# Column sums of squares: sixteen accumulating matmuls or vector additions and one matmul, and the order of the first weight split

## The chip, the cores and the metric

The kernel runs on one core of a Trainium2 chip. The metric is the device time of one execution in microseconds (us), the median of repeated runs. Five engines run side by side, each through its own list of instructions: TensorE (PE) multiplies matrices into the accumulation banks (PSUM, eight banks), VectorE (DVE) and ScalarE (ACT) work element by element, GpSimd (POOL) too, and SyncE (SP) issues the transfers. They wait for each other by semaphores alone. The profile tells a matmul (PE) from the load of its stationary operand (PEld).

## The reference, cut to what matters

Two layers of a decoder trunk, for a prompt of 1024 tokens and 8 sample tokens, so 1032 token columns in all; model width 1024, hidden width 2816:

```
def rmsnorm(x, g):
    y = x * lax.rsqrt(jnp.mean(x * x, axis=-1, keepdims=True) + EPS)
    return y * g

for layer in range(2):
    h = rmsnorm(x, norm_mix_pre[layer])
    mix = mixer(h) @ w_out                       # layer 0: gMLP and DeltaNet, layer 1: differential attention
    x = x + rmsnorm(mix, norm_mix_post[layer])
    h = rmsnorm(x, norm_ffn_pre[layer])
    f = (gelu(conv(h @ w_gate) + b) * (h @ w_up)) @ w_down
    x = x + rmsnorm(f, norm_ffn_post[layer])
```

Activations are kept transposed, width on the 128 partitions (8 row blocks of 128) and tokens along the free dimension. So the mean over the width in `rmsnorm` is a sum over partitions: a matmul of the squares with a matrix of ones, here called a column sum. It leaves the sum in each of the 128 partitions.

## The kernel before

All of it is written engine by engine: the order of each engine's instructions is the order of the code, and no scheduler moves anything. The 1032 tokens are cut into three thirds of 344 columns (`CH`). Each product of 32-bit matrices is made of three matmuls, high half by high half, high by low and low by high; so each operand is split once into a rounded copy (`..._hi`, ScalarE) and the remainder (`..._lo`, VectorE).

The diff touches one function, `stage_out_ffn`, which runs once per layer. Its parts:

1. The output projection of the mixer. `out_unit(c, m)` makes one 128 x 344 unit (third c, row block m) from 24 matmuls. Before it the input and the weights are split: `input_hi` and `input_lo` take one block of one third, `weight_hi` and `weight_lo` one weight tile of 128 x 1024. The first unit waits for weight tile 0 and, block by block, for the input.
2. Both norms and the gate and up projections of the first group, then eleven groups of the hidden width in a loop.
3. The last group, by thirds. `end_unit(n)` makes unit n (n = 0 to 23, eight per third) of the down projection from 6 matmuls; `end_collect(n)` adds it on VectorE to the sum in `T.acc`; `end_square(n)` squares it on ScalarE; `end_sum(n)` is its column sum, three units later (`LAG`), accumulated over the eight blocks. `end_root(c)` makes the reciprocal root on ScalarE (a logarithm and an exponential, each with a load of its function table), and `end_renew(c, k)` on VectorE scales block k and adds the old x, two instructions.
4. In layer 0 alone (`queries is not None`): the next norm and the query projection of layer 1. `end_square_x` squares the new x, `end_sum_x` takes its column sums, `end_root2` the root; `end_input(c)` scales and splits a third (a scaling and a remainder per block on VectorE, the copy `end_hi` on ScalarE), and `query(q)` makes unit q of 24 from 24 matmuls. `move_query(q)` empties its bank. Queries 8 to 15 read the second third, 16 to 23 the last.
5. In layer 1 alone (`closing`): `turn_out` transposes the result on TensorE, ScalarE copies it out of PSUM and SyncE stores it. This is the end of the kernel.

A column sum of 344 columns stands in the program as one matmul of `T.con` (the ones) with a square; in the trace it has two rows of PE (L1222). Each of the 24 units of part 3 has such a sum, and each of the 24 blocks of part 4.

## Time and profile before

| | us |
|---|---|
| runs | 3087.94, 3082.85, 3080.01 |
| median | 3082.85 |
| the profiled execution | 3086.49 |
| its span, first to last instruction | 3084.7 |
| TensorE busy | 2900.4 |
| VectorE busy | 1522.8 |
| ScalarE busy | 1034.2 |

The page of the profile gives the busy time of each engine and, in 40 slices of about 77 us, where it is busy. TensorE is at 9 tenths or more in most slices, and its granted clock (a share of full speed, 2.4 GHz) has a mean of 0.97. The end of layer 0 (parts 3 and 4) lies from 1528 to 1678 us of the span, the end of layer 1 from 3023 us to the last instruction; the two output projections begin at 680 and 2175 us. In a timeline the first number is the start in us from the start of the span, the second the time in us, then engine, line and operation with its operands, and in square brackets the idle time before it and what ended that.

### The profile page before, as it was taken

The numbers are of one execution on the slowest core, as the hardware profiler recorded it, in microseconds if no ns is written. First come the engines' busy times: TensorE is split into PE (matmuls) and PEld (weight loads), VectorE is DVE, ScalarE is ACT, GpSimd is POOL, SyncE is SP. The second block draws the span as 40 slices with busy tenths as digits, with TensorE's granted clock in tenths as the row PEclk, the third lists the DMA queues.
The fourth block names the chain that finished last, engine by engine and source line by source line (L and its number), as shares of the span: only waits on it lengthen the run. The fifth ranks groups of instructions, "written<-read, shape, count | busy, mean of one in ns | idle before, by whom it ended". The sixth has DMA issues, their size and how long they took to land. (4 is left out here: it accounts for less than half of the span.)

```text
span 3084.7 us, 46174 instructions
## 1 busy us (share of the span) xinstructions
PE 2900.4 (94%) x18588; PEld 2775.9 (90%) x18588; DVE 1522.8 (49%) x2258; ACT 1034.2 (34%) x1747; POOL 586.7 (19%) x322
## 2 busy tenths in 40 slices
PE   6999989969999999999998999996899999999997
PEld 5999888849899999999978888885899999999996
DVE  3067333356744444444471576773566444444435
ACT  3326544335511111111261566663462111111114
POOL 1122135200222222222100121210003222222210
PEclk8999989969999999999999999997999999999999
DMA  4111100043311111111131222213431111111103
GB/s 151 47 43 30 38 1 0 1 112 107 108 55 41 41 41 41 54 54 48 37 110 37 62 84 76 69 55 125 130 109 42 56 52 54 41 41 41 41 14 112
DMA packets 183498, 185.02 MB, mean 60 GB/s; under 512 B 10469, under 2 KB 168549, under 8 KB 183296
## 3 DMA queue, kind: packets, MB, share of 16 engines
q1 hardware_dynamic: 183380, 183.45, 19.0%
q8 instruction: 74, 1.21, 0.2%
q14 instruction: 44, 0.36, 0.0%
HBM read 151.13 MB, written 32.57 MB: 60 GB/s over the span
## 5 line engine op out<-in xcount | busy, mean ns | idle before, releaser
L1530 DVE TENSOR_TENSOR acc<-acc,ps 128x1032 f32<-128x1032 f32 x144 | 177.0, 1229 | 231.9 <-PE ps L124 231.9
L1911 PE MATMUL ps<-mix_in0hi,in0wh 128*128 128x344 f32 x600 | 197.8, 330 | 14.9 <-POOL mix_in0lo L244 9.1
L124 PE MATMUL ps<-midlo,rest0wh 128*128 128x344 f32 x984 | 209.3, 321 | 0.0
L124 PE MATMUL ps<-mix_out1lo,rest1wh 128*128 128x344 f32 x984 | 209.2, 321 | 0.0
L124 PE MATMUL ps<-midhi,rest0wl 128*128 128x344 f32 x984 | 208.8, 321 | 0.0
L124 PE MATMUL ps<-mix_out1hi,rest1wh 128*128 128x344 f32 x984 | 208.7, 320 | 0.0
L124 PE MATMUL ps<-midhi,rest0wh 128*128 128x344 f32 x984 | 208.7, 320 | 0.0
L124 PE MATMUL ps<-mix_out1hi,rest1wl 128*128 128x344 f32 x984 | 208.6, 320 | 0.0
L1911 PE MATMUL ps<-mix_in0hi,in0wl 128*128 128x344 f32 x600 | 193.1, 322 | 0.0
L1911 PE MATMUL ps<-mix_in0lo,in0wh 128*128 128x344 f32 x600 | 193.1, 322 | 0.0
L124 PEld LDWEIGHTS ps<-midhi,rest0wl 128*128 128x128 f32 x984 | 165.7, 188 | 0.0
L124 PEld LDWEIGHTS ps<-mix_out1hi,rest1wl 128*128 128x128 f32 x984 | 165.6, 188 | 0.0
L124 PEld LDWEIGHTS ps<-mix_out1lo,rest1wh 128*128 128x128 f32 x984 | 165.5, 188 | 0.0
L124 PEld LDWEIGHTS ps<-midhi,rest0wh 128*128 128x128 f32 x984 | 165.5, 188 | 0.0
L124 PEld LDWEIGHTS ps<-midlo,rest0wh 128*128 128x128 f32 x984 | 165.4, 188 | 0.0
L124 PEld LDWEIGHTS ps<-mix_out1hi,rest1wh 128*128 128x128 f32 x984 | 165.4, 188 | 0.0
L2884 PE MATMUL ps<-midhi,at_wh 128*128 128x344 f32 x384 | 133.1, 347 | 20.0 <-POOL at_wl L3252 9.2
L1911 PEld LDWEIGHTS ps<-mix_in0hi,in0wh 128*128 128x128 f32 x600 | 114.0, 190 | 18.5 <-issue 9.0
L383 POOL TENSOR_TENSOR rest0wl<-wraw,rest0wh 128x1024 fp32r<-128x1024 f32 x40 | 96.4, 2410 | 165.7 <-ACT rest0wh L379 165.5
L383 POOL TENSOR_TENSOR rest1wl<-wraw,rest1wh 128x1024 fp32r<-128x1024 f32 x40 | 96.1, 2404 | 166.4 <-ACT rest1wh L379 166.1
L2884 PE MATMUL ps<-midlo,at_wh 128*128 128x344 f32 x384 | 124.5, 324 | 0.0
L2884 PE MATMUL ps<-midhi,at_wl 128*128 128x344 f32 x384 | 124.5, 324 | 0.0
(496 smaller groups left out, 7060.7 us busy)
## 6 DMA issues: line engine op xcount, KB each, us to landing
wraw<-in_w_ffn_gate SPq DMA_DIRECT2D x22, 1024.0 KB, 5.1
wraw<-in_w_ffn_up SPq DMA_DIRECT2D x22, 1024.0 KB, 5.1
wraw<-in_w_ffn_down SPq DMA_DIRECT2D x22, 1024.0 KB, 4.8
wraw<-x_scratch SPq DMA_DIRECT2D x96, 172.0 KB, 3.1
x_scratch<-acc SPq DMA_DIRECT2D x72, 172.0 KB, 3.1
wraw<-in_w_in_even SPq DMA_DIRECT2D x24, 512.0 KB, 3.8
wraw<-in_w_in_odd SPq DMA_DIRECT2D x24, 512.0 KB, 4.8
sr_page<-in_cache_k SPq DMA_DIRECT2D x16, 512.0 KB, 4.0
```

The lines of the kernel that those rows point to most:

```text
L124: ins = pe.matmul(ps[:, 3 * r + c, 0:CH], w, h[:, c * CH:(c + 1) * CH], start=first and n == 0, stop=last and n == 2)
L383: pool.tensor_tensor(self.slot_l[j], self.source(j), self.slot_h[j], ALU.subtract).then_inc(self.lo[j], 1)
L1530: dve.tensor_tensor(a, a, region(T.ps, m % 2), ALU.add).then_inc(collected, 1)
L1911: ins = pe.matmul(bank(n, c), w[n % 2][:, k, :], cut(h[:, k, :], c), start=first and m == 0, stop=final and m == 2)
L2884: ins = pe.matmul(unit_bank, x[b][:, k, :], y[:, k, c * CH:(c + 1) * CH], start=k == 0 and m == 0, stop=k == KD - 1 and m == 2)
```

## The change

Three things are changed.

First, the squares of the first two thirds of the down projection (parts 3, both layers) are no longer summed by eight accumulating matmuls each. ScalarE writes the square of block 0 into a buffer `sum1[c]`, VectorE adds the squares of blocks 1 to 7 to it (`end_add`), and TensorE makes one column sum, `end_sum(0)` after unit 10 and `end_sum(1)` after unit 19. The last third keeps its eight sums, now called `end_last`.

Second, the same for the second and third third of the next norm in layer 0 (`end_add_x`, then `end_sum_x(1)` after query 4 and `end_sum_x(2)` after query 10; before they stood, eight each, after queries 3 and 6). The first third keeps its eight sums (`end_first_x`); its last one now stands ahead of the last three of `end_last`. On ScalarE and VectorE the squares, the weight splits and the moves around them are put in another order.

Third, in the output projection of both layers the first weight tile is split ahead of the input, and the second after input block 3.

A branch that no call takes (`not by_thirds`) is removed with its helper objects.

```diff
-            x_sq = [sum1[0], sum1[1]] + end_sq
+            x_sum, x_sq = [None, end_sq[0], end_sq[1]], [end_sq[2], end_sq[3], sum1[0], sum1[1]]
+            x_first = scaled
...
             @block.scalar
                 def end_square(n):
                     c, m = divmod(n, KD)
                     act.wait_ge(moved, NX + n + 1)
-                    if n >= 4:
-                        act.wait_ge(post_made, 3 + n - 3)
-                    act.activation(end_sq[n % 4], cut(T.acc, m, c), ACT.Square).then_inc(squared, 1)
+                    if c < 2 and m == 0:
+                        dst = sum1[c]
+                    else:
+                        dst = end_sq[n % 4]
...
+                        elif n >= 4:
+                            act.wait_ge(added, 21 + adds_until(n - 4))
+                    act.activation(dst, cut(T.acc, m, c), ACT.Square).then_inc(squared, 1)
...
+                weight_hi(0)
                 for k in range(KD):
                     input_hi(k, 0)
-                weight_hi(0)
-                weight_hi(1)
+                    if k == 3:
+                        weight_hi(1)
...
                     for k in range(KD):
                         end_hi(0, k)
+                    for k in range(4):
+                        end_square_x(1, k)
                     for m in range(4, KD):
                         query_hi(m)
+                    for k in range(4, KD):
+                        end_square_x(1, k)
                     end_root(2)
-                    for k in range(KD):
-                        end_square_x(1, k)
-                    for q in range(3):
+                    for q in range(2):
                         move_query(q)
                     end_root2(1)
...
             @block.tensor
+                def end_sum(c):
+                    if c == 0:
                         pe.wait_ge(keep_moved, 6)
+                    pe.wait_ge(added, 21 + 7 * c + 7)
+                    ones(end_post[c], sum1[c]).then_inc(post_made, 1)
...
+                def end_sum_x(c):
+                    pe.wait_ge(rooted2, 3 + c)
+                    pe.wait_ge(x_added, X_ADDS + 7 * c)
+                    ones(second, x_sum[c]).then_inc(second_made, 1)
...
+                for n in range(NX):
+                    end_unit(n)
+                    if n == 10:
+                        end_sum(0)
+                    if n == 19:
+                        end_sum(1)
+                    if n >= 2 * KD + LAG:
+                        end_last(n - 2 * KD - LAG)
+                    if queries is not None and n > 2 * KD:
+                        end_first_x(n - 2 * KD - 1)
                 if queries is not None:
-                    end_sum_x(0, KD - 1)
+                    end_first_x(KD - 1)
+                for m in range(KD - LAG, KD):
+                    end_last(m)
+                if queries is not None:
                     for q in range(NX):
                         query(q)
-                        if q in (3, 6):
-                            for k in range(KD):
-                                end_sum_x(q // 3, k)
+                        if q == 4:
+                            end_sum_x(1)
+                        if q == 10:
+                            end_sum_x(2)
...
             @block.vector
+                def end_add(n):
+                    c, m = divmod(n, KD)
+                    if m == 0:
+                        return
+                    dve.wait_ge(squared, NX + n + 1)
+                    if m > 1:
+                        dve.wait_ge(added, 21 + 7 * c + m - 1)
+                    dve.tensor_tensor(sum1[c], sum1[c], end_sq[n % 4], ALU.add).then_inc(added, 1)
...
+                weight_lo(0)
                 for k in range(KD):
                     input_lo(k, 0)
-                weight_lo(0)
-                weight_lo(1)
+                    if k == 3:
+                        weight_lo(1)
...
+                for n in range(2 * KD):
+                    end_collect(n)
+                    if n >= LAG:
+                        end_add(n - LAG)
+                for k in range(KD):
+                    end_renew(0, k)
+                    end_collect(2 * KD + k)
+                    if k < LAG:
+                        end_add(2 * KD - LAG + k)
...
+                    for k in range(1, 4):
+                        end_add_x(1, k)
                     for m in range(4, KD):
                         query_lo(m)
-                    for k in range(KD):
+                    for k in range(4, KD):
+                        end_add_x(1, k)
+                    for k in range(5):
                         end_renew(2, k)
                     end_input(1)
+                    for k in range(5, KD):
+                        end_renew(2, k)
+                    for k in range(1, KD):
+                        end_add_x(2, k)
                     end_input(2)
```

How the rows move, at three places. TensorE in layer 0, last group, before: a column sum (L1222; the squares lie in `ffn0gate`) after each unit of six matmuls (L1305, the last of one unit and all of the next are shown).

```order
L1305 MATMUL ps<-rest0wh,rest0wl 128x344
L1222 MATMUL ps<-ffn0gate,con_sb 128x344 [waits ev_cv_moved]
L1305 MATMUL ps<-rest0wh 128x344 [waits ev_cv_turned]
L1305 MATMUL ps<-rest0wl,rest0wh 128x344
L1305 MATMUL ps<-rest0wh,rest0wl 128x344
L1305 MATMUL ps<-rest0wh 128x344
L1305 MATMUL ps<-rest0wl,rest0wh 128x344
L1305 MATMUL ps<-rest0wh,rest0wl 128x344
L1222 MATMUL ps<-ffn0conv,con_sb 128x344 [waits ev_cv_moved]
```

The same place now, around unit 10: the end of unit 10, the one sum of the first third (L1224, of `sqsum`, where `sum1` lies), unit 11 (L1307) and the start of unit 12.

```order
L1307 MATMUL ps<-rest0wh,rest0wl 128x344
L1224 MATMUL ps<-sqsum,con_sb 128x344 [waits ev_mixed_made,ev_w_masked]
L1307 MATMUL ps<-rest0wh 128x344 [waits ev_turned]
L1307 MATMUL ps<-rest0wl,rest0wh 128x344
L1307 MATMUL ps<-rest0wh,rest0wl 128x344
L1307 MATMUL ps<-rest0wh 128x344
L1307 MATMUL ps<-rest0wl,rest0wh 128x344
L1307 MATMUL ps<-rest0wh,rest0wl 128x344
L1307 MATMUL ps<-rest0wh 128x344 [waits ev_turned]
```

No sum stands between units 11 and 12 now; the one that is left waits for VectorE's additions, where each of before waited for ScalarE's square.

VectorE at the same stage, before: `end_collect` (L1553), then the renewals (L1560, L1563).

```order
L1590 TENSOR_TENSOR rest0wl<-wraw,rest0wh 128x1024 [waits gd_s_updated1] x2
L1553 TENSOR_TENSOR acc<-acc,ps 128x344 [waits ev_mix_own] x16
L1560 TENSOR_TENSOR acc<-acc,ffn0conv 128x344 [waits ev_n_summed]
L1563 SCALAR_TENSOR_TENSOR acc<-acc,gain,wraw 128x344 [waits ev_n_logged,ev_col_in]
L1553 TENSOR_TENSOR acc<-acc,ps 128x344 [waits ev_mix_own]
L1560 TENSOR_TENSOR acc<-acc,ffn0conv 128x344
```

And now, from the last collections of the second third on (L1564 collects, L1573 adds a square, L1586 and L1589 renew).

```order
L1564 TENSOR_TENSOR acc<-acc,ps 128x344 [waits ev_v_normed]
L1573 TENSOR_TENSOR sqsum<-sqsum,ffn0gate 128x344 [waits ev_mixed_made,ev_vt_moved]
L1586 TENSOR_TENSOR acc<-acc,ffn0conv 128x344 [waits ev_mix_own]
L1589 SCALAR_TENSOR_TENSOR acc<-acc,gain,wraw 128x344 [waits ev_cv_turned,ev_n_summed]
L1564 TENSOR_TENSOR acc<-acc,ps 128x344 [waits ev_v_normed]
L1573 TENSOR_TENSOR sqsum<-sqsum,ffn0gate 128x344 [waits ev_mixed_made,ev_vt_moved]
L1586 TENSOR_TENSOR acc<-acc,ffn0conv 128x344
```

After each collection there is now an addition, also between the first three renewals and the next collection.

VectorE at the start of the output projection of layer 0, before: eight input remainders of the first third (L1444), then three weight remainders (L1547).

```order
L1440 UNCONDITIONAL_BRANCH [waits barrier_Pool_Activation_PE_DVE_SP_release]
L1444 TENSOR_TENSOR midlo<-acc,midhi 128x344 [waits ev_mixed_made] x8
L1547 TENSOR_TENSOR rest0wl<-wraw,rest0wh 128x1024 [waits ev_turned] x3
L1444 TENSOR_TENSOR midlo<-acc,midhi 128x344 [waits ev_mixed_made] x2
L1451 COPY acc<-ps 128x344 [waits ev_mix_moved,ev_mix_own]
```

And now (L1558 is the weight remainder, L1455 that of the input).

```order
L1451 UNCONDITIONAL_BRANCH [waits barrier_Pool_Activation_PE_DVE_SP_release]
L1558 TENSOR_TENSOR rest0wl<-wraw,rest0wh 128x1024 [waits ev_v_squared]
L1455 TENSOR_TENSOR midlo<-acc,midhi 128x344 [waits ev_v_logged] x4
L1558 TENSOR_TENSOR rest0wl<-wraw,rest0wh 128x1024 [waits ev_v_squared]
L1455 TENSOR_TENSOR midlo<-acc,midhi 128x344 [waits ev_v_logged] x4
L1558 TENSOR_TENSOR rest0wl<-wraw,rest0wh 128x1024 [waits ev_v_squared]
```

The same three weight remainders and eight input remainders stand there, with one weight remainder ahead of the first input block; ScalarE's copies are ordered alike.

## Rows read from the trace of the kernel before

**Rows 1.** the page, part 1: busy time of each engine
```profile
PE 2900.4 (94%) x18588; PEld 2775.9 (90%) x18588; DVE 1522.8 (49%) x2258; ACT 1034.2 (34%) x1747; POOL 586.7 (19%) x322
```

**Rows 2.** timeline of TensorE, queries of layer 0; start us, busy us, what
```profile
1593.04 1.32 PE L1222 MATMUL ps<-sqsum,con_sb 128*128 128x344 f32 x4
1594.19 1.90 PE L1222 MATMUL ps<-ffn0gate,con_sb 128*128 128x344 f32 x6
```

**Rows 3.** timeline of VectorE, last group of layer 0
```profile
1529.23 0.51 DVE L1553 TENSOR_TENSOR acc<-acc,ps 128x344 f32<-128x344 f32 x1
1530.17 0.51 DVE L1553 TENSOR_TENSOR acc<-acc,ps 128x344 f32<-128x344 f32 x1 [0.43 <-PE ps L1305]
...
1533.59 0.52 DVE L1553 TENSOR_TENSOR acc<-acc,ps 128x344 f32<-128x344 f32 x1 [1.01 <-PE ps L1305]
1535.12 0.51 DVE L1553 TENSOR_TENSOR acc<-acc,ps 128x344 f32<-128x344 f32 x1 [1.01 <-PE ps L1305]
...
1550.77 0.51 DVE L1560 TENSOR_TENSOR acc<-acc,ffn0conv 128x344 f32<-128x344 f32 x1
...
1551.86 0.51 DVE L1553 TENSOR_TENSOR acc<-acc,ps 128x344 f32<-128x344 f32 x1
1552.29 0.51 DVE L1560 TENSOR_TENSOR acc<-acc,ffn0conv 128x344 f32<-128x344 f32 x1
...
1566.70 0.51 DVE L1553 TENSOR_TENSOR acc<-acc,ps 128x344 f32<-128x344 f32 x1 [1.17 <-PE ps L1305]
...
1572.55 0.58 DVE L1573 SCALAR_TENSOR_TENSOR ffn0spare<-acc,gain,sqsum 128x344 f32<-128x344 f32 x1 [1.19 <-ACT sqsum L141]
```

**Rows 4.** timeline of ScalarE, last group of layer 0
```profile
1567.24 0.49 ACT L1025 ACTIVATE ffn0conv<-acc 128x344 f32<-128x344 f32 x1 [0.91 <-DVE acc L1553]
1567.75 1.28 ACT L140 ACT_TABLE_LOAD   x1
1570.17 0.55 ACT L140 ACTIVATE sqsum<-ps,eps 128x344 f32<-128x344 f32 x1 [1.13 <-PE ps L1222]
...
1572.03 0.49 ACT L141 ACTIVATE sqsum<-sqsum 128x344 f32<-128x344 f32 x1
```

**Rows 5.** timeline of TensorE, first query of layer 0
```profile
1574.35 0.48 PE L1338 MATMUL ps<-midhi,rest0wh 128*128 128x344 f32 x1 [4.22 <-DVE midlo L1578]
```

**Rows 6.** timeline of ScalarE, later queries of layer 0
```profile
1632.67 0.46 ACT L1066 ACTIVATE acc<-ps 128x344 f32<-128x344 f32 x1 [3.31 <-PE ps L1338]
```

**Rows 7.** who waited for whom, 1527 to 1700 us: total, times, longest
```profile
DVE ffn0spare L1573 <- ACT sqsum L141: 10.3, 3, 7.4
```

**Rows 8.** timeline of VectorE, last group of layer 1
```profile
3024.05 0.51 DVE L1553 TENSOR_TENSOR acc<-acc,ps 128x344 f32<-128x344 f32 x1 [2.72 <-PE ps L1305]
...
3057.34 0.51 DVE L1553 TENSOR_TENSOR acc<-acc,ps 128x344 f32<-128x344 f32 x1
```

**Rows 9.** timeline of ScalarE, start of the output projection of layer 0
```profile
679.88 3.15 ACT L904 ACTIVATE midhi<-acc 128x344 fp32r<-128x344 f32 x8 [16.59 <-PEq L2682]
...
692.64 1.04 ACT L908 ACTIVATE rest0wh<-wraw 128x1024 fp32r<-128x1024 f32 x1
```

**Rows 10.** timeline of VectorE, the same stretch
```profile
684.01 3.50 DVE L1547 TENSOR_TENSOR rest0wl<-wraw,rest0wh 128x1024 fp32r<-128x1024 f32 x3
...
693.72 1.23 DVE L1547 TENSOR_TENSOR rest0wl<-wraw,rest0wh 128x1024 fp32r<-128x1024 f32 x1 [1.51 <-ACT rest0wh L908]
694.86 0.94 DVE L1444 TENSOR_TENSOR midlo<-acc,midhi 128x344 fp32r<-128x344 f32 x2
...
720.20 1.16 DVE L1457 TENSOR_TENSOR sqsum<-sqsum,ffn0gate 128x344 f32<-128x344 f32 x2
```

**Rows 11.** timeline of TensorE, the same stretch
```profile
685.29 0.66 PE L1237 MATMUL ps<-midhi,rest0wh 128*128 128x344 f32 x1 [14.26 <-DVE rest0wl L1547]
...
690.05 0.49 PE L1237 MATMUL ps<-midlo,rest0wh 128*128 128x344 f32 x1
690.33 0.38 PE L1237 MATMUL ps<-midhi,rest0wl 128*128 128x344 f32 x1
```

More of the change, by code:

```diff
@@ L758, in stage_out_ffn @@
         was_scaled, n_hi, n_lo, x_out, act_own = sem("was_scaled"), sem("n_hi"), sem("n_lo"), sem("x_out"), sem("act_own")
-        by_thirds = closing is not None or queries is not None
+        X_ADDS = 14
         BANKS, LAG = (6, 3) if queries is None else (5, 3)
@@ L764, in stage_out_ffn @@
         end_bank = lambda n: T.ps[:, bank_of(n), 0:CH]
+        adds_until = lambda n: 7 * (n // KD) + n % KD
         end_sq = [third(gate[:, 2:2 + TOK], n) for n in range(3)] + [third(conv, 0)]
@@ L851, in _ @@
                 sp.wait_ge(x_out, 16 * NX)
-                if not by_thirds:
-                    sp.wait_ge(keep_moved, 1)
-                    sp.dma_start(out_prompt[layer, 0], kept_rows[0:2, :]).then_inc(out_done, 16)
-                    sp.dma_start(out_sample[layer, :, 1, :], kept_rows[2:KEEP, :]).then_inc(out_done, 16)
-                    sp.wait_ge(out_done, 48)
-                else:
-                    if queries is not None:
-                        for j in range(feed.SLOTS):
-                            sp.wait_ge(lo[j], GROUPS)
-                        queries.first(sp)
-                    sp.wait_ge(keep_moved, 6)
-                    for cols, src in rows:
-                        sp.dma_start(out_prompt[layer, 0][:, cols], src[0:2, :]).then_inc(out_done, 16)
-                        sp.dma_start(out_sample[layer, :, 1, cols], src[2:KEEP, :]).then_inc(out_done, 16)
-                    sp.wait_ge(out_done, 80)
-                    for n in range(4):
-                        load_end_x(n)
+                if queries is not None:
+                    for j in range(feed.SLOTS):
+                        sp.wait_ge(lo[j], GROUPS)
+                    queries.first(sp)
+                sp.wait_ge(keep_moved, 6)
+                for cols, src in rows:
+                    sp.dma_start(out_prompt[layer, 0][:, cols], src[0:2, :]).then_inc(out_done, 16)
+                    sp.dma_start(out_sample[layer, :, 1, cols], src[2:KEEP, :]).then_inc(out_done, 16)
+                sp.wait_ge(out_done, 80)
+                for n in range(4):
+                    load_end_x(n)
                 if queries is not None:
@@ L1212, in _ @@
                 group(GROUPS - 1, False)
-                if not by_thirds:
-                    pool.memset(T.sqsum[:], 0.0).then_inc(sqsum_own, 1)
-                    for m in range(KD):
-                        squares.gpsimd(pool, m // 2, m % 2, lambda: pool.wait_ge(
-                            *((squares.summed[(m - 1) % 2], (m + 1) // 2) if m else (sqsum_own, 1))))
             @block.tensor
@@ L1403, in _ @@
                 pe.wait_ge(gate_in, 2 * GROUPS)
-                if by_thirds:
-                    pe.wait_ge(multiplied, 2 * GROUPS)
-                else:
-                    down(GROUPS - 1, 2 * GROUPS)
-                    pe.wait_ge(collected, KD * GROUPS)
+                pe.wait_ge(multiplied, 2 * GROUPS)
                 pe.wait_ge(kept, 2 * GROUPS)
@@ L1650, in _ @@
                     group(g, True)
-                if not by_thirds:
-                    collect(GROUPS - 1)
-                    dve.wait_ge(keep_turned, 1)
-                    dve.tensor_copy(kept_rows, flat[:, 0:FF]).then_inc(keep_moved, 1)
-                else:
-                    if queries is not None:
-                        query_lo(2)
-                        query_lo(3)
-                    for n in range(2 * KD):
-                        end_collect(n)
-                    for k in range(KD):
-                        end_renew(0, k)
-                        end_collect(2 * KD + k)
+                if queries is not None:
+                    query_lo(2)
+                    query_lo(3)
+                for n in range(2 * KD):
[7 more added lines that the diff above has]
+                        end_add(2 * KD - LAG + k)
                 if queries is not None:
```

107 lines of the change are left out of this document (52 added, 55 removed).

## The prediction

> **What bounds the kernel now.** I read the page first, then the timeline of each engine alone in the four stretches that the change touches, then the waits of the second half of layer 0. On the page TensorE is busy 94% of the span and VectorE 49% [rows 1]: time taken off TensorE counts wherever no other engine takes its place. What one column sum costs TensorE is to be read from starts, since recorded times overlap: four rows of L1222 take 1594.19 - 1593.04 = 1.15 us, so a row is 0.289 us and a sum of two rows 0.58 us [rows 2]. In the last group VectorE's collections follow TensorE's units: 1530.17 - 1529.23 = 0.94 us apart while no sum stands between, 1.52 us once one does, each with about 1 us of VectorE idle until TensorE is done [rows 3]. So there TensorE sets the pace and VectorE has room.
>
> **The first two thirds of the last group (both layers).** Removed: 16 sums, added 2, in each layer. Added on VectorE: 14 additions of 344 columns per layer. The trace has that operation beside a collection: from 1551.86 to 1552.29 the next instruction starts 0.43 us after a collection, while its recorded time is 0.51 us [rows 3]. I price collection plus addition at 2 x 0.43 = 0.86 us, under TensorE's 0.94. The bounds of one addition are 0.43 us and the 1.16 - 0.51 = 0.65 us by which the second of two dependent additions ends behind the first elsewhere; I take 0.43, since here a collection stands between two additions. The Trainium skill ("VectorE: DVE Perf Modes", Terms) says that a flush follows every VectorE operation and the next can't issue until the pipe is empty. By that rule a pair would cost 1.02 us and the units would be paced by VectorE; the rows' 0.43 us between starts says that most of the recorded tail is overlapped, and the measurement decides.
>
> Now the chain, counted from the start of the first collection. Before, the renewals begin at 1550.77 - 1529.23 = 21.5 us [rows 3]. After: 15 units of 0.945 are 14.2 us; the sum of the first third stands behind unit 10 and waits for the addition of block 7, which VectorE makes after collecting unit 10. TensorE stands there for one collection and one addition (0.43 + 0.51) and hand-overs of some 0.2 us (estimate), 1.2 us, and then needs 0.58. The last collection and addition take 0.86. Sum 16.8 us: 4.7 us earlier. Squares of units 11 to 15 wait behind ScalarE's root as before and are in time for their additions.
>
> **The last third, layer 0.** Before, from the first renewal to the last collection: 1566.70 - 1550.77 = 15.9 us [rows 3]. A renewal (two instructions) and a collection take VectorE 1552.29 - 1550.77 = 1.52 us. Now the first three steps hold an addition too, 1.95 us each, and the sum of the second third (behind unit 19) waits for the last of these, at 5.9 us. From there TensorE has three sums (1.7 us), three units with two sums each (0.94 + 1.16 = 2.1 us each, 6.3), the last unit (0.94), 0.6 us for the root of the second third that holds up ScalarE's squares, and 0.2 to the collection: 15.7 us. So only 0.2 us is gained: what the missing sums save, the wait for VectorE takes.
>
> Behind the last collection ScalarE squares, loads a table, takes the logarithm, loads, takes the exponential, and VectorE begins the next input 5.85 us after the collection. In it ScalarE waits 1.13 us for TensorE's last sum, since sums of the down projection stand ahead of it [rows 4]. Now that sum stands ahead of them and is made while the table is loaded; the chain is 0.54 + 0.49 + 1.28 + 0.56 + 1.30 + 0.52 = 4.7 us, 1.1 us less. The pause of TensorE ahead of the first query (4.22 us) [rows 5] shrinks a little and takes the three moved sums. Layer 0 reaches its queries 4.7 + 0.2 + 1.1 = 6.0 us earlier.
>
> **The queries of layer 0.** 24 units of 24 matmuls, 3.31 + 0.46 = 3.77 us each [rows 6], TensorE never waiting after the first one. Sixteen sums become two: 14 x 0.58 = 8.1 us, if the later thirds are in time. VectorE gets 14 more additions, back to back, at most 0.65 us each, 9.1 us. Against them stand 10.3 us in which it waited here for ScalarE's root, 7.4 at once ahead of the last third [rows 7]. Worked through: the second third's squares are summed some 4 us before query 4 ends; sum 0.6 and root 2.5 us later VectorE makes the second input, its first block 7 us before query 8 reads it and its last (8.5 us later) while query 8 runs, which needs that block only at its end. The last third has about 5 us to spare at query 10. I cost the reordering on ScalarE at nothing: its moves of queries stay within the five banks by one query or more at every place.
>
> **The last third, layer 1.** The last collection comes at 3057.34 - 3024.05 = 33.3 us, the next renewal 0.43 later, 33.7 [rows 8]. No sum of a next norm stands here, and VectorE is the pace of this third already (1.52 us per step, no idle time). After: 16.8 us as above, three steps of 1.95 and five of 1.52: 30.3 us. Gain 3.4 us, though TensorE is relieved of 8.1. ScalarE's last root, the copies out and the stores hang on the last collection and move with it.
>
> **The first weight tile (both layers).** ScalarE's first copy starts at 679.88; a weight copy takes 1.04 us and hands over 1.08 us after its start [rows 9]. VectorE makes three weight remainders at 684.01, behind eight input remainders; one weight remainder holds it for 694.86 - 693.72 = 1.14 us [rows 10]. TensorE starts at 685.29, 5.41 us after ScalarE [rows 11]. Now: 1.08 (weight copy), 1.14 (weight remainder), 0.52 (first input remainder), 0.05: 2.8 us, so 2.6 us earlier. Behind it: the second weight remainder comes after input block 3, so block 4 is ready 2.9 us after the first; TensorE, slow here, needs three matmuls of 690.33 - 690.05 = 0.28 us per block [rows 11], 3.4 us for four, and does not catch up. SyncE's transfer of weight tile 4, which waits for the first remainder, is issued about 3 us earlier, behind the six small loads that stand ahead of it. The total work of VectorE and ScalarE up to unit 1 is the same, and TensorE is the pace of the rest of this part, so the lead lasts. The bounds are 0 and 2.6 us; the value is the second, as every handed-over time has a row. Layer 1 begins alike: 2 x 2.6 = 5.2 us.
>
> TensorE's clock: the first matmuls here run at the lower level (1.2 GHz), until about 690.3, 5.0 us after the first, behind a pause of 14 us [rows 11]. If the rise stays at its old moment instead of moving with the first matmul, the 2.6 us that are won run at half speed and are worth 1.3. The Trainium skill ("TensorE: Matmul & The Clock Gate", Part 1) calls the half rate the default that activity releases: by that rule the rise moves along, and the sum stays.
>
> **Sum.** 6.0 + 8.1 + 3.4 + 5.2 = 22.7 us. The profiled execution took 3086.49 us with a span of 3084.7, so its like would be 3063.8 and 3062.0. It is 3.6 us above the median of the runs (3082.85); against the median the forecast is 3060.2 us, 0.7% faster.
>
> **The rivals.**
>
> A, VectorE becomes the pace of the first two thirds: an addition costs 0.65 us instead of 0.43. For: the two dependent additions at 720.20 [rows 10]. Against: they stand back to back. Price: pair 1.08 us against 0.945 on 13 units and 0.22 in three steps, 2.4 us per layer: gain 17.9, time 3065.
>
> B, the early first tile gives half or nothing (clock, or a wait behind it): 2.6 to 5.2 us less, 3062.8 to 3065.4.
>
> C, a later third is late at query 8 or 16, because VectorE or ScalarE is held up (a store or load of x, a table load): TensorE waits there. For: fourteen additions and a longer chain ahead of the input. Against: the slack above. Price up to the 8.1 us of that term: 3068.
>
> D, the other side: the new pauses of TensorE (1.2 us behind unit 10, 0.8 and 0.4 ahead of the first two sums of the next norm, 0.8 behind unit 19) let its clock fall at the end of layer 0 and it is not raised again before the queries are through. A query then takes 24 x 0.28 = 6.8 us instead of 3.8. It decides from 22.7 / 3.0 = 7.6 queries at the lower level; over all 24 it costs 72 us, time 3132. Against: behind the far longer pause of 14 us the lower level lasted 5.0 us [rows 11], and the pause ahead of the first query that is there already, 4.22 us [rows 5], is longer than any new one and no query behind the first is slow [rows 6].
>
> E, it doesn't do what it says: the sums' time was hidden somewhere I took for exposed, and half of the gain is missing or less: 3071 to 3083. Against: the 1.52 against 0.94 us of rows 3.
>
> **Chances.** The forecast (3057 to 3063) 0.66, A 0.10, B 0.08, C 0.06, D 0.03, E 0.04, more than forecast (all 42 removed sums count, 24.3 + 5.2 = 29.5 us, 3053) 0.03. The range is 3053 to 3069: from that bound up to C with the scatter of the runs. Less than 0.3% (9.2 us) can hardly be told from no change here; faster than that are all cases but D, E and a part of C: 0.92. Within it 0.05, slower 0.03.
>
> **What would show it.** The collections of units 1 to 10 start 0.95 us apart, with under 0.1 us of VectorE idle between; a single pause of TensorE of about 1.2 us ahead of the sum of the first third; the next input begins 4.7 us after the last collection; no idle time of TensorE from query 1 on, and its busy time about 24 us lower; the first matmul 2.8 us after ScalarE's first copy; from first to last collection in layer 1 29.9 us instead of 33.3. Wrong would be: collections 1.1 us apart (A), a pause ahead of query 8 or 16 (C), a granted clock under 0.9 in the queries (D).

## The result, and the profile after

The changed kernel takes 3059.34 us (median of 4 runs, 3056.90 to 3064.17), the kernel before 3082.56 us on the same chip (4 runs, 3080.01 to 3087.94). The ratio is 0.9925 (95% interval 0.9912 to 0.9937), 0.75% faster; the forecast was 3060.2 us. A second set of 5 runs gave 3058.11 us, ratio 0.9927 (0.9914 to 0.9941). The profiled execution has a span of 3062.3 us, against 3084.7 before.

The page's first part (engine, busy us, share of the span, instructions) answers to [rows 1]:

```profile
PE 2877.0 (94%) x18504; PEld 2759.3 (90%) x18504; DVE 1539.4 (50%) x2300; ACT 1033.4 (34%) x1747; POOL 586.7 (19%) x322
```

TensorE is busy 23.4 us less, VectorE 16.6 us more. The shares hardly move; where the time went is seen only in the stages.

The last group of layer 0, from VectorE's timeline (start, duration, engine, line, operation; in brackets the idle time before and what ended it). L1564 is a collection, L1573 an addition, L1586 the first half of a renewal, L1599 the scaling that begins the next input. It answers to [rows 3].

```profile
1527.67 0.51 DVE L1564 TENSOR_TENSOR acc<-acc,ps 128x344 f32<-128x344 f32 x1 [0.17 <-PE ps L1307]
...
1536.23 0.51 DVE L1564 TENSOR_TENSOR acc<-acc,ps 128x344 f32<-128x344 f32 x1
1536.66 0.51 DVE L1573 TENSOR_TENSOR sqsum<-sqsum,ffn0gate 128x344 f32<-128x344 f32 x1
1537.16 0.51 DVE L1564 TENSOR_TENSOR acc<-acc,ps 128x344 f32<-128x344 f32 x1
1537.59 0.51 DVE L1573 TENSOR_TENSOR sqsum<-sqsum,ffn0conv 128x344 f32<-128x344 f32 x1
1540.05 0.51 DVE L1564 TENSOR_TENSOR acc<-acc,ps 128x344 f32<-128x344 f32 x1 [1.95 <-PE ps L1307]
...
1544.67 0.51 DVE L1586 TENSOR_TENSOR acc<-acc,ffn0conv 128x344 f32<-128x344 f32 x1
...
1546.56 0.51 DVE L1586 TENSOR_TENSOR acc<-acc,ffn0conv 128x344 f32<-128x344 f32 x1
...
1560.42 0.51 DVE L1564 TENSOR_TENSOR acc<-acc,ps 128x344 f32<-128x344 f32 x1 [1.20 <-PE ps L1307]
...
1565.16 1.06 DVE L1599 SCALAR_TENSOR_TENSOR ffn0spare<-acc,gain,sqsum 128x344 f32<-128x344 f32 x2
```

From the fifth collection on there is one every 0.94 us with an addition between, and VectorE is not idle; the pace is still TensorE's (a collection starts within 0.05 us of the end of its unit's last matmul). Then comes one hole, in which TensorE waited for the addition of block 7 (1537.59) and made the sum and unit 11. TensorE's timeline has that pause, and the two that matter later:

```profile
1538.25 0.82 PE L1224 MATMUL ps<-sqsum,con_sb 128*128 128x344 f32 x2 [1.12 <-DVE sqsum L1573]
...
1566.95 0.39 PE L1348 MATMUL ps<-midhi,rest0wh 128*128 128x344 f32 x1 [3.09 <-DVE midlo L1604]
...
3028.16 0.84 PE L1224 MATMUL ps<-sqsum,con_sb 128*128 128x344 f32 x2 [2.92 <-DVE sqsum L1573]
```

ScalarE at the end of that group, and at the last query, answers to [rows 4] and [rows 6]. The root (L140) no longer waits for a sum: no bracket stands behind it.

```profile
1560.97 0.49 ACT L1026 ACTIVATE ffn0conv<-acc 128x344 f32<-128x344 f32 x1 [0.91 <-DVE acc L1564]
1561.48 1.28 ACT L140 ACT_TABLE_LOAD   x1
1562.77 0.55 ACT L140 ACTIVATE sqsum<-ps,eps 128x344 f32<-128x344 f32 x1
...
1613.40 0.55 ACT L140 ACTIVATE sqsum<-ps,eps 128x344 f32<-128x344 f32 x1 [4.98 <-PE ps L1224]
...
1662.43 0.46 ACT L1072 ACTIVATE acc<-ps 128x344 f32<-128x344 f32 x1 [3.31 <-PE ps L1348]
```

The output projection of layer 0: ScalarE's first copy, VectorE's first remainder, TensorE's first and first fast matmul, VectorE's first collection. It answers to [rows 9 to 11].

```profile
681.18 1.06 ACT L903 ACTIVATE rest0wh<-wraw 128x1024 fp32r<-128x1024 f32 x1 [16.58 <-PEq L2716]
682.27 1.22 DVE L1558 TENSOR_TENSOR rest0wl<-wraw,rest0wh 128x1024 fp32r<-128x1024 f32 x1 [5.75 <-ACT rest0wh L903]
684.07 0.63 PE L1239 MATMUL ps<-midhi,rest0wh 128*128 128x344 f32 x1 [11.73 <-DVE midlo L1455]
688.23 0.38 PE L1239 MATMUL ps<-midhi,rest0wl 128*128 128x344 f32 x1
690.05 0.52 DVE L1462 COPY acc<-ps 128x344 f32<-128x344 f32 x1
```

The last group of layer 1 on VectorE (first collection, first renewal, last collection), against [rows 8]:

```profile
3005.36 0.51 DVE L1564 TENSOR_TENSOR acc<-acc,ps 128x344 f32<-128x344 f32 x1 [2.73 <-PE ps L1307]
...
3022.36 0.51 DVE L1586 TENSOR_TENSOR acc<-acc,ffn1conv 128x344 f32<-128x344 f32 x1
...
3035.13 0.51 DVE L1564 TENSOR_TENSOR acc<-acc,ps 128x344 f32<-128x344 f32 x1
```

Stage by stage, in us, each from one mark to the next in the two traces:

| stage | before | after | gain | forecast |
|---|---|---|---|---|
| layer 0, ScalarE's first copy to first collection of the last group | 849.35 | 846.49 | 2.86 | 2.6 |
| layer 0, that collection to the next input | 43.32 | 37.49 | 5.83 | 6.0 |
| layer 0, next input to last query's move | 105.39 | 97.27 | 8.12 | 8.1 |
| layer 1, first copy to first collection of the last group | 849.21 | 846.27 | 2.94 | 2.6 |
| layer 1, first to last collection | 33.29 | 29.77 | 3.52 | 3.4 |

The five gains are 23.3 us (forecast 22.7). What isn't in the table was not changed: layer 0's projection begins 1.3 us later than before (681.18 against 679.88), attention is 0.24 us shorter, the end 0.14. 23.3 - 1.3 + 0.4 = 22.4 us, the difference of the spans.

### The profile page after: what moved, and what is told of

It reads as the page before. It is cut to its first block and busy times, and to the rows that moved or that the text cites. A ratio compares the mean times of both kernels' runs of the same rounds, so it can differ in the third digit from the quotient of the medians.

```text
span 3062.3 us, 46088 instructions
## 1 busy us (share of the span) xinstructions
PE 2877.0 (94%) x18504; PEld 2759.3 (90%) x18504; DVE 1539.4 (50%) x2300; ACT 1033.4 (34%) x1747; POOL 586.7 (19%) x322
## 5 line engine op out<-in xcount | busy, mean ns | idle before, releaser
L2918 PE MATMUL ps<-midhi,at_wh 128*128 128x344 f32 x384 | 132.7, 346 | 22.4 <-ACT at_vin L3044 11.3
```

Source lines behind the costliest of these rows:

```text
L2918: ins = pe.matmul(unit_bank, x[b][:, k, :], y[:, k, c * CH:(c + 1) * CH], start=k == 0 and m == 0, stop=k == KD - 1 and m == 2)
```

## The experiments

Every kernel below was timed in 5 rounds (the second addition in 3), and its ratio is to the kernel before on the same chip. The ratios carry an uncertainty of about 0.15%, 4 to 5 us. Differences smaller than that are read from marks in the traces, inside a stage, where the same stage of two profiled executions of the changed kernel agrees within 0.1 us. Across the untouched parts they don't: these two executions have spans of 3062.3 and 3054.1 us, and most of the 8 us lie between the last query of layer 0 and layer 1's projection (496.7 against 490.1 us).

**The first weight tile alone**, on the kernel before (ScalarE; VectorE's part is alike):

```diff
+                weight_hi(0)
                 for k in range(KD):
                     input_hi(k, 0)
-                weight_hi(0)
-                weight_hi(1)
+                    if k == 3:
+                        weight_hi(1)
```

> The kernel before with only the first weight tile split ahead of the input, on ScalarE and on VectorE, in both layers. My theory: TensorE's first matmul comes 2.6 to 2.9 us earlier behind ScalarE's first copy in each layer and the lead lasts, 5.2 to 5.9 us in all, so about 3077 us (ratio 0.998). Rival B (the early tile gives half or nothing, since the rise of TensorE's clock keeps its moment or a wait stands behind): 3080 to 3083, ratio 0.999 to 1.000.

Measured: 3077.18 us, ratio 0.9979 (0.9970 to 0.9988). From ScalarE's first copy to the first collection of the last group the trace has 846.61 us in layer 0 and 846.38 in layer 1, 2.74 and 2.83 less than before, 5.6 in all. The theory holds and rival B falls: the lead lasts over more than 800 us. What becomes of the clock's rise when the first matmul comes sooner is taken up again with the halves below.

**The changed kernel without it:** the same lines taken back.

> The changed kernel with the input split ahead of the first weight tile again, as before. My theory: it loses the 5.2 to 5.9 us of the early tile and nothing else, about 3065 us (ratio to the kernel before 0.9942), and the parts add up: its gain and that of the early tile alone sum to the whole gain of 23.2 us. Rival B: no slower than the changed kernel, 3059 to 3062. A rival for the sum: the parts overlap, and the two gains add up to clearly more or less than 23 us.

Measured: 3067.84 us, ratio 0.9952 (0.9939 to 0.9966). By the medians it loses 8.5 us, more than expected but within the uncertainty; by the trace 2.91 us in layer 0 (849.40 against 846.49 us). The gains of the two parts (6.3 and 15.6 us) sum to 21.9 us, against 23.2 us for the whole: within the uncertainty they add up.

**The query sums again:**

```diff
                         if q == 10:
                             end_sum_x(2)
+                        if q in (4, 10):
+                            for _ in range(7):
+                                ones(end_post[1], T.con[:, 0:CH])
```

> The changed kernel, with seven column sums more on TensorE behind each of queries 4 and 10 of layer 0 (of constants, into a bank that nobody reads): TensorE gets back the 14 sums that the change took from the queries, while VectorE keeps its additions. My theory: TensorE is the pace of the queries throughout, each sum is 0.58 us, so 8.1 us slower than the changed kernel, 3067.5. Rival C (VectorE's chain of additions, root and input is late somewhere, so that TensorE waited there anyway): less than 8.1 us is lost, about 3 to 6. Rival E (the sums had been hidden): 3059 to 3062.

Measured: 3071.79 us, ratio 0.9962 (0.9949 to 0.9976). The two marks in its trace, VectorE's next input and ScalarE's last move of a query:

```profile
1565.63 1.07 DVE L1602 SCALAR_TENSOR_TENSOR ffn0spare<-acc,gain,sqsum 128x344 f32<-128x344 f32 x2
...
1671.01 0.46 ACT L1072 ACTIVATE acc<-ps 128x344 f32<-128x344 f32 x1 [3.31 <-PE ps L1348]
```

105.38 us, where the changed kernel has 97.27 and the kernel before had 105.39. The 14 sums cost 8.11 us, 0.58 each, wholly exposed: rivals C and E fall. The median lost 12 us (11 by the two ratios); what goes beyond 8.1 lies in untouched parts (2.1 us of it in the profiled execution, between the queries and layer 1) or in the scatter.

**One more addition on VectorE**, eleven times in each layer:

```diff
+                    if n <= 12:
+                        dve.tensor_tensor(scaled[n % 2], end_sq[n % 4], end_sq[n % 4], ALU.add)
                     dve.tensor_tensor(sum1[c], sum1[c], end_sq[n % 4], ALU.add).then_inc(added, 1)
```

> The changed kernel with one more addition of 344 columns on VectorE (its result is used by nobody) ahead of each of eleven additions in the first two thirds of the last group, in both layers. My theory (an addition holds VectorE for 0.43 us, and a pair with a collection just fits under TensorE's 0.945 us): a step becomes 3 x 0.43 = 1.29 us, VectorE is the pace, eleven steps lose 0.345 us each, 3.8 us per layer, and the pause ahead of the first sum grows by 0.4: about 8.4 us slower than the changed kernel, 3068. Rival A (an addition costs 0.65 us): steps of 1.5 us or more, at least 6.5 us per layer, 3072 or more.

Measured: 3072.47 us, ratio 0.9959 (0.9945 to 0.9973). VectorE's timeline shows the pace (L1574 is the extra addition), and TensorE's what came with it:

```profile
1530.83 0.50 DVE L1564 TENSOR_TENSOR acc<-acc,ps 128x344 f32<-128x344 f32 x1
1531.25 0.51 DVE L1574 TENSOR_TENSOR ffn0spare<-ffn0gate 128x344 f32<-128x344 f32 x1
1531.68 0.51 DVE L1575 TENSOR_TENSOR sqsum<-sqsum,ffn0gate 128x344 f32<-128x344 f32 x1
1532.10 0.50 DVE L1564 TENSOR_TENSOR acc<-acc,ps 128x344 f32<-128x344 f32 x1
```

```profile
1538.72 0.82 PE L1224 MATMUL ps<-sqsum,con_sb 128*128 128x344 f32 x2 [3.53 <-DVE sqsum L1575]
...
1539.93 0.49 PE L1307 MATMUL ps<-rest0wh 128*128 128x344 f32 x1
...
1543.28 0.32 PE L1307 MATMUL ps<-rest0wh 128*128 128x344 f32 x1
```

The addition is what I priced: a step is 1532.10 - 1530.83 = 1.27 us, three times 0.425. So rival A's 0.65 us is wrong here. But the kernel lost 13 us by the median (10 by the two ratios) and 12.4 by the trace (first to last collection 5.7 and 6.7 us longer), not 8.4, so the expected sum fell, though the price of an addition held. The pause ahead of the first sum grew from 1.12 to 3.53 us, not by 0.4: VectorE fell behind by a third of a microsecond per unit while TensorE ran ahead through its free banks. That is where the loss of the first seven steps shows, and not a loss on top of it.

What my sum lacked is the clock. Behind this pause it fell to the lower level for 3.4 us (0.49 us records, from 1539.9 on). The trace has four such stretches that the changed kernel has not, each 3.4 us long: in layer 0 also from 1550.0, behind a pause of 1.89 us, and in layer 1 from 3024.5 and from 3038.2, behind pauses of 3.53 and 4.00 us. First collection to first renewal takes 5.1 us longer in either layer instead of 4.2, and the rest up to the last collection 0.6 and 1.6 us longer instead of nothing: these are the 4 us beyond the expected. That they are the clock's is argued from where they lie; no run separates them here. It is rival D in small.

**The sums one unit later:**

```diff
-                    if n == 10:
+                    if n == 11:
                         end_sum(0)
-                    if n == 19:
+                    if n == 20:
                         end_sum(1)
-                    if n >= 2 * KD + LAG:
-                        end_last(n - 2 * KD - LAG)
+                    if n > 2 * KD + LAG:
+                        end_last(n - 2 * KD - LAG - 1)
...
-                for m in range(KD - LAG, KD):
+                for m in range(KD - LAG - 1, KD):
                     end_last(m)
```

> The changed kernel with the sum of the first third behind unit 11 instead of unit 10, and that of the second third behind unit 20 instead of 19 (the last third's sums one unit later too). My theory: TensorE no longer stands 1.1 us ahead of the first sum, nor 0.4 us ahead of the second in layer 0, and the first renewal comes 0.9 to 1.1 us earlier in both layers: 2 to 2.5 us in all, 3057 us (0.999 of the changed kernel). Rival: the pause isn't removed but moved, because ScalarE's squares of units 12 to 15 now wait behind a root that comes as late as before while the sum itself is no earlier, or VectorE's pace in the last third takes the lead back: 3059, no change.

Measured: 3058.43 us, ratio 0.9918 (0.9905 to 0.9932); against the changed kernel that is no difference that the times can show. The trace can. VectorE's timeline (unit 12, first renewal, last collection), and TensorE's first sum:

```profile
1538.49 0.51 DVE L1564 TENSOR_TENSOR acc<-acc,ps 128x344 f32<-128x344 f32 x1 [1.44 <-PE ps L1307]
...
1542.17 0.51 DVE L1586 TENSOR_TENSOR acc<-acc,ffn0conv 128x344 f32<-128x344 f32 x1
...
1557.29 0.51 DVE L1564 TENSOR_TENSOR acc<-acc,ps 128x344 f32<-128x344 f32 x1 [1.49 <-PE ps L1307]
```

```profile
1536.69 0.82 PE L1224 MATMUL ps<-sqsum,con_sb 128*128 128x344 f32 x2 [0.18 <-DVE sqsum L1573]
```

With the first collection at 1526.11, the first renewal comes after 16.06 us instead of 17.0 and the last collection after 31.18 instead of 32.75; the pause is 0.18 instead of 1.12 us. Layer 1's group takes 28.61 instead of 29.77 us. In all 2.6 us, of which 1.5 are left at layer 0's next input. The theory holds.

**Early matmuls:** TensorE gets three matmuls on constants at the head of each output projection.

```diff
+                for _ in range(2):
+                    ones(post, T.con[:, 0:CH])
+                ones(post[:, 0:P], T.con[:, 0:P])
                 for m in range(KD):
                     out_unit(0, m)
```

> The changed kernel, with three matmuls on constants (two of 344 columns, one of 128, into a bank whose content is overwritten later) on TensorE at the head of each layer's output projection, where it would stand idle for 2.9 us until the first block of the input is ready. In the changed kernel the first matmuls run at the lower clock level for 4.2 us from the first one. My theory on the clock (the rise follows TensorE's first work and not a fixed moment): the rise now comes some 2.8 us earlier, when only 1.4 us of the real work has been done; unit 0 is then limited by VectorE's input remainders and is collected 0.5 to 1.0 us earlier, 1 to 2 us in all, about 3058 us. Rival B, in its form that the rise keeps its moment whatever TensorE does: slow matmuls until the same moment, nothing gained, 3059 to 3060.

Measured: 3056.76 us, ratio 0.9906 (0.9888 to 0.9924). TensorE's timeline:

```profile
680.24 3.06 PE L1224 MATMUL ps<-con_sb 128*128 128x344 f32 x6 [8.88 <-PEq L2719]
683.11 0.62 PE L1239 MATMUL ps<-midhi,rest0wh 128*128 128x344 f32 x1
683.53 0.49 PE L1239 MATMUL ps<-midlo,rest0wh 128*128 128x344 f32 x1
683.82 0.36 PE L1239 MATMUL ps<-midhi,rest0wl 128*128 128x344 f32 x1
...
685.86 0.43 PE L1239 MATMUL ps<-midhi,rest0wh 128*128 128x344 f32 x1 [0.28 <-DVE midlo L1458]
```

The records are short from 683.8 on, 0.7 us after the first real matmul and 3.6 us after the first of all; in the changed kernel it was 4.2 us after the first real one. The rise follows TensorE's work here, as I had assumed against rival B. The Trainium skill ("TensorE: Matmul & The Clock Gate", Part 1) has it that activity releases the full rate, and this trace agrees. The stage up to the last group's first collection is 843.87 us in layer 0 and 843.63 in layer 1, 2.6 us shorter in each. I had expected at most 1.0. Of it 1.0 us is the head: the transposes behind unit 1 start 11.5 us after ScalarE's first copy instead of 12.5 (unit 0 itself is collected only 0.1 us sooner, where I had expected 0.5 to 1.0). The rest appears 105 us later, ahead of the last post norm's sum, where TensorE waits 2.22 us in both kernels. Behind that pause the changed kernel runs 3.4 us at the lower level, and this one does not.

**The pause filled:** the changed kernel, with three sums of constants in just that pause.

```diff
                 first_unit(0, 0).then_inc(first_made, 1)
+                pe.wait_ge(rooted1, 2)
+                for _ in range(3):
+                    ones(post, T.con[:, 0:CH])
                 post_sum(2)
```

> The changed kernel with three column sums of constants on TensorE (1.7 us, into the bank of the post norm's sum, which the real sum overwrites) in the pause of 2.22 us ahead of the last post norm's sum of the output projection, in both layers. In the changed kernel a stretch of 3 us at the lower clock begins right behind that pause; in the two kernels with matmuls at the projection's head the same pause stood without such a stretch. If the pause is what lets the clock fall: no slow stretch behind it, and the first collection of the last group comes 1.5 us sooner behind ScalarE's first copy in each layer, 3 us in all, 3056. If something from the head of the projection decides it and not the pause: the slow stretch stays, 3059.

Measured: 3058.13 us, ratio 0.9924 (0.9911 to 0.9938), the same as the changed kernel in its group. Busy time by stretch (stretch, its length, busy us and instructions of PE, PEld, DVE, ACT and POOL, then the granted clock as a share of full speed, DMA share, GB/s), first of the changed kernel, then of this one, in layer 0 behind the pause:

```profile
786.00:788.00 2.00, 1.28 (x4) 1.02 (x5) 1.97 (x5) 0.98 (x2) 0.00 (x0) 0.83 0.00 0
788.00:790.00 2.00, 2.00 (x8) 2.00 (x8) 1.83 (x5) 1.23 (x3) 0.00 (x0) 0.50 0.00 0
790.00:792.00 2.00, 2.00 (x12) 2.00 (x12) 0.30 (x1) 1.95 (x4) 0.00 (x0) 0.82 0.00 0
```

```profile
784.00:786.00 2.00, 1.52 (x9) 1.30 (x9) 1.96 (x6) 0.98 (x2) 0.00 (x0) 1.00 0.00 0
786.00:788.00 2.00, 2.00 (x14) 2.00 (x13) 1.83 (x4) 1.43 (x4) 0.00 (x0) 1.00 0.00 0
```

The stage is 844.89 and 844.73 us, 1.6 and 1.5 less than in the changed kernel: the stretch at half speed is gone, and with it the loss, as the theory said. But 1.6 us were given back in layer 1's last group, which takes 31.36 instead of 29.77 us. There the sum of the second third waits 2.92 us for VectorE in both kernels, and in this one the clock is at the lower level when the wait ends (from 3020.8 to 3024.2). TensorE's next sum behind it in the changed kernel (0.74 us recorded for two rows, 0.68 us after the sum that waited), and then the same place of this one (1.35 us, 1.31 us after):

```profile
3028.84 0.74 PE L1224 MATMUL ps<-ffn1gate,con_sb 128*128 128x344 f32 x2
```

```profile
3020.91 1.52 PE L1224 MATMUL ps<-sqsum,con_sb 128*128 128x344 f32 x2 [2.92 <-DVE sqsum L1576]
3022.22 1.35 PE L1224 MATMUL ps<-ffn1gate,con_sb 128*128 128x344 f32 x2
3022.87 0.99 PE L1307 MATMUL ps<-rest1wh 128*128 128x344 f32 x1
```

The kernel with the early matmuls did the same there (31.38 us). So the same wait costs nothing in one program and 1.6 us in another.

**The first weight tile in halves** (ScalarE; VectorE's part is alike, and TensorE waits for the second half at block 4):

```diff
-                weight_hi(0)
-                for k in range(KD):
+                act.wait_ge(w_in[0], 16)
+                act.activation(w_h[0][:, 0:4, :], w_raw[0][:, 0:4, :], ACT.Copy).then_inc(w_hi0, 1)
+                input_hi(0, 0)
+                act.activation(w_h[0][:, 4:8, :], w_raw[0][:, 4:8, :], ACT.Copy).then_inc(w_hi, 1)
+                for k in range(1, KD):
```

> The changed kernel with the first output weight tile split in two halves of four blocks, the first half ahead of the first input block and the second behind it, on ScalarE and on VectorE; TensorE waits for the second half only at block 4. My theory: the first matmul comes 1.1 us earlier in each layer (half a weight copy and half a remainder), but VectorE's blocks 1 and 4 then come late for TensorE, which gets there sooner: 0.4 to 1.1 us of it is left per layer, 3057.5 to 3058.5 us. Rival: VectorE's total work up to block 4 is the bound and nothing is left, 3059.3.

Measured: 3061.99 us, ratio 0.9922 (0.9907 to 0.9937), no difference by the times. TensorE starts 1.93 us behind ScalarE instead of 2.89, and the stage is 845.97 and 845.74 us: 0.5 of the 1.0 us is left in each layer. ScalarE's first copy, TensorE's first and first fast matmul:

```profile
679.22 0.63 ACT L1076 ACTIVATE rest0wh<-wraw 128x512 fp32r<-128x512 f32 x1 [16.59 <-PEq L2728]
681.15 0.63 PE L1247 MATMUL ps<-midhi,rest0wh 128*128 128x344 f32 x1 [10.78 <-DVE midlo L1463]
686.27 0.37 PE L1247 MATMUL ps<-midhi,rest0wl 128*128 128x344 f32 x1
```

The size is as expected, the reason is not. TensorE comes 0.1 us late at block 1 and at no block behind it. But the clock rises 7.05 us behind ScalarE's first copy (686.27 - 679.22), exactly as in the changed kernel (688.23 - 681.18): the first matmul came 1.0 us sooner and the rise did not, so the time that was won was spent at half speed. In this small step rival B's mechanism is what happened.

**Together:** the later sums, the halves and two early matmuls.

> The changed kernel with the later sums (first third behind unit 11, second behind unit 20), the first weight tile in halves, and two matmuls on constants at the head of each output projection. If the three small gains are independent: 2.7 us from the later sums by the trace, 1 to 2 from the halves, up to 1 from the earlier rise of the clock, so 3054 to 3056 us. Rival: the halves and the early matmuls both end at VectorE's remainders of blocks 4 to 7 and give nothing beyond the later sums, 3057.

Measured: 3052.26 us, ratio 0.9892 (0.9874 to 0.9909), faster than either expected. The stage up to the last group is 843.59 and 843.37 us, 2.9 us shorter in each layer: the transposes behind unit 1 start 1.3 us sooner, and the stretch at the lower clock behind the 2.22 us is gone here too; the last groups keep what the later sums gave (31.18 and 28.60 us).

**The later sums with three early matmuls, no halves:**

> The changed kernel with the later sums (first third behind unit 11, second behind unit 20) and three matmuls on constants at the head of each output projection, without the halved first tile. By the traces of the two alone: 2.7 us from the later sums and 5.3 us from the early matmuls, so 3051 to 3052 us; the kernel that had the halves as well took 3052.3. Rival: the halves carry part of that gain and it stays at 3054 or more.

Measured: 3052.53 us, ratio 0.9906 (0.9891 to 0.9921). By the median the rival falls; the ratios (0.9892 with the halves, on another chip) differ by 4 us, within their uncertainty, and can't tell. Both kernels beat the kernel before by 1%, and the changed kernel by about 6 us (this one ran from 3050.02 to 3056.20, the changed one in the same group from 3055.87 to 3063.62). Their last group of layer 1 takes 28.6 us, without a slow stretch: with the later sum TensorE waits 1.98 us there, not 2.92. By the trace the halves carry 0.3 us per layer (843.59 and 843.37 us against 843.85 and 843.63), so little that the rival falls by it.

**The changed kernel again:**

> The changed kernel once more, as a measure for the others of this group: 3059 us, ratio 0.992 to 0.993 to the kernel before. Its traces should differ from the first one only ahead of layer 0's output projection and in the attention between the layers.

Measured: 3058.11 us, the ratio above. As expected, its stages are those of the first trace (846.17 us for layer 1's first stage, 29.78 for its last group).

## Why the prediction was right

**First two thirds.** The pair of collection and addition comes every 0.94 us, at TensorE's pace; the doubled additions show that each takes 0.425 us, so a pair could be made in 0.85. From first collection to first renewal it is 17.0 us in both layers, 16.8 forecast; the pause is 1.12 instead of 1.2 us. One line of "what would show it" was loose: only from the fifth collection on is VectorE without idle time, because the additions begin three units behind. Before that it waits 0.44 us each time.

**Last third, layer 0.** 15.75 us from first renewal to last collection, 15.7 forecast. The steps with an addition take 1.89, not 1.95 us: the addition itself is 0.43 us as priced, but the collection now starts 0.49 us after the renewal's second instruction, where it was 0.55 in the steps that I took as a base. Why is open. TensorE's wait ahead of the second sum is 0.42 us (0.8 in rival D).

**Tail.** From the last collection to the next input 4.74 us, 4.7 forecast. ScalarE's wait for the sum is gone.

**Queries.** 8.12 us, 8.1 forecast, and the same 8.11 when the sums are put back. VectorE's last addition of the last third ended at 1608.7 and TensorE's sum began at 1612.6: 3.9 us to spare where I said 5. For the second third it was 3.1 (1586.4 to 1589.4) where I said some 4, and its input's first block was ready 6.8 us before query 8 (7 forecast). Back to back the additions start 0.62 us apart, within the bound of 0.65. No pause of TensorE is left from query 1 on.

**Last third, layer 1.** 29.8 us, 29.9 forecast.

**First weight tile.** 2.9 us per layer instead of 2.6: this term was mis-sized. The first matmul came 2.89 us behind ScalarE's first copy (2.8 forecast), so 2.5 us were won there; the rest is the clock. It rose 4.2 us after the first matmul instead of 5.0, and 0.9 us less at half speed is another 0.4 us. I had let the rise move along with the first matmul, at its old distance. It doesn't keep one: behind ScalarE's first copy it came 3.4 us sooner for a first matmul 2.5 us sooner, and with the halves not at all sooner for another 1.0 us. So what the clock adds to such a gain was not in my sum, and the runs give it only case by case.

**The rivals.** A fell with the changed kernel's own steps of 0.94 us and with the doubled additions, B with the tile alone and the early matmuls, C and E with the sums put back. D did not happen in the changed kernel in a way that costs: in the first query the clock does fall, from 1569.0 to 1572.4, as it did before (1574.5 to 1577.9), but VectorE's blocks set that query's pace: in the kernel with later sums and early matmuls the clock doesn't fall there, and the queries take 97.26 us from mark to mark, against 97.27. The other kernels show that D's mechanism is there and takes 1.6 us a time where TensorE is the pace. It doesn't last, so its price of 72 us was far too high. My list of new pauses was one of layer 0 and lacked the longest, 2.92 us in layer 1.

**How much is luck.** The stages agree with their forecasts within 0.2 us, the tile's within 0.4, by the mechanisms that were named; the first two thirds took 0.2 us more than forecast and the tile won 0.3 us more in each layer, so the errors partly cancel. That the medians agree within 0.9 us is more than the method can promise: the runs of this one kernel spread over 7 us.

What stays open is why the clock falls behind one pause and not behind an equal one. Behind the 2.22 us ahead of the last post norm's sum, it fell in the kernel before, in the changed one and in all others that left the pause and gave TensorE nothing to do ahead of the projection (the halves too); with early matmuls it didn't, 100 us later and with the pause unchanged, though it comes 1.0 us sooner there behind the head, so that its moment may count as well as the matmuls. Behind the 2.92 us in layer 1 it fell in two kernels, and not in the changed one or in three others. It fell behind 1.89 us in one kernel and behind 1.98 us in none of three. The length of the pause alone doesn't decide, and no run here separates what does.

## What to carry to other kernels

A reduction by ones on the busiest engine can be folded on an engine that has gaps, if each fold fits between two steps of the pace: compare start-to-start spacing, not recorded lengths. Place the single sum that is left one unit behind the step that delivers its last operand, or the pacing engine stands for it; at the head of a stage, order the splits by what the first matmul needs. Read such a change in stages, from mark to mark: there 0.1 us can be told, while whole executions of one and the same kernel differed here by 8 us.

## What the runs showed of the hardware

- VectorE starts its next operation 0.425 us after an addition of 128 x 344 numbers if that is not waiting for anything, while each is recorded as 0.51 us long; so also three in a row. Where an addition needs the result of the one just ahead, the spacing is 0.62 us. The Trainium skill ("VectorE: DVE Perf Modes", Terms) says that the next operation can't issue until the pipe is empty; the measured spacing is shorter than the recorded length.
- TensorE ran at the lower level (0.49 instead of 0.32 us records) for 3.4 us at a time behind pauses of 2.22 us (most kernels), 2.92 us (two kernels) and, with the doubled additions, 1.89, 3.53 and 4.00 us, and never behind 1.12 us. Such a stretch cost 1.6 us where TensorE was the pace, and nothing in the first query, where VectorE was.
- Behind ScalarE's first copy, three matmuls on constants that ran 2.9 us ahead of the real work brought the clock's rise 3.4 us sooner, and behind a pause 100 us later no slow stretch followed in the three kernels that had such matmuls. Real work that began 1.0 us sooner (the halves) left the rise where it was.
